# The later modulation units as pairs of half contractions by 512 columns, in another order of the weight stream

## The reference

```
m = silu(cond) @ w_mod + b_mod                    # w_mod is 1024 x 6144
shift1, scale1, gate1, shift2, scale2, gate2 = split(m, 6)
h = rmsnorm(x, g_mix) * (1 + scale1) + shift1
... = split(h @ w_in)                             # inputs of four token mixers
branches = [retention, window attention, differential attention, latent attention]
branches = einsum('blnc,ncd->blnd', branches, w_branch)      # n: the mixer
gates = sigmoid(h @ w_gate + b_gate)                         # 4 x 1024 columns
mixed = sum(gates * branches, axis=mixer) @ w_out
x = x + gate1 * mixed
h2 = rmsnorm(x, g_ffn) * (1 + scale2) + shift2
x = x + gate2 * mlp(h2)                           # gated, with a convolution of width 3
```

## Time and profile before

| what | value |
| --- | --- |
| median of 3 runs | 2319.7 us (2318.75 to 2321.82) |
| profiled execution, its own time | 2321.85 us |
| its span | 2319.7 us |
| busy: PE, PEld, DVE, ACT, POOL | 99%, 89%, 55%, 40%, 32% of the span |
| moved by DMA | 221.62 MB, 96 GB/s on the mean |

### The profile page before, as it was taken

One profiled execution on the slowest core, in us unless ns is written; L12 is line 12 of the kernel. 1 busy time (PEld: TensorE's weight loads), 2 busy tenths in 40 slices (PEclk: granted clock), 3 DMA queues, 4 the chain that ended last, 5 costly groups with the idle time before them and its releaser, 6 DMA issues.

```text
span 2319.7 us, 40593 instructions
## 1 busy us (share of the span) xinstructions
PE 2287.5 (99%) x17116; PEld 2062.1 (89%) x17116; DVE 1275.7 (55%) x2234; ACT 924.5 (40%) x1763; POOL 750.1 (32%) x498
## 2 busy tenths in 40 slices
PE   7999999999999999999999999999999999999998
PEld 5888898888989998998988879888889899899897
DVE  4436458644336763763664373685444467547556
ACT  3335346634335331331362452555442443223223
POOL 0331221211433544544422303121123435544442
PEclk9999999999999999999999999999999999999999
DMA  9413222223242324223232142222232322222211
GB/s 317 139 57 121 76 95 81 78 74 107 100 127 73 91 91 128 73 91 123 78 137 75 39 134 92 85 67 92 74 110 84 108 91 74 76 70 78 87 60 68
DMA packets 221906, 221.62 MB, mean 96 GB/s; under 512 B 10582, under 2 KB 191390, under 8 KB 221470
## 3 DMA queue, kind: packets, MB, share of 16 engines
q1 hardware_dynamic: 212999, 193.77, 26.2%
q10 hardware_dynamic: 8727, 25.27, 3.2%
HBM read 209.90 MB, written 9.11 MB: 94 GB/s over the span
## 4 chain that ended last, share of the span: by engine, by line
PE 93%; DVE 3%; ACT 3%; issue 1%; POOL 1%; DMA 0%; SPq 0%; POOLq 0%; DVEq 0%; ACTq 0%
PE ps L896 50%; PE ps L1027 12%; PE ps L1564 11%; PE ps L1486 4%; PE ps L1168 3%; PE ps L1185 2%; PE ps L916 2%; PE ps L1129 1%; PE ps L1144 1%; PE ps L992 1%; PE ps L1114 1%; PE ps L1388 1%; PE ps L1150 1%; PE ps L907 1%; POOL w_lo L855 1%
## 5 line engine op out<-in xcount | busy, mean ns | idle before, releaser
L855 POOL TENSOR_TENSOR w_lo<-raw,w_hi 128x512 fp32r<-128x512 f32 (+1 forms) x486 | 739.9, 1552 | 1547.6 <-ACT w_hi L1636 992.8
L896 PE MATMUL ps<-h_hi,w_hi 128*128 128x320 f32 (+2 forms) x2368 | 615.2, 312 | 0.0
L896 PE MATMUL ps<-h_hi,w_lo 128*128 128x320 f32 (+2 forms) x2368 | 607.2, 309 | 0.0
L896 PE MATMUL ps<-h_lo,w_hi 128*128 128x320 f32 (+2 forms) x2368 | 606.6, 309 | 0.0
L896 PEld LDWEIGHTS ps<-h_hi,w_hi 128*128 128x128 f32 x2368 | 413.4, 188 | 7.1 <-issue 4.6
L896 PEld LDWEIGHTS ps<-h_lo,w_hi 128*128 128x128 f32 x2368 | 413.4, 188 | 0.2
L896 PEld LDWEIGHTS ps<-h_hi,w_lo 128*128 128x128 f32 x2368 | 412.9, 188 | 0.0
L1636 ACT ACTIVATE w_hi<-raw 128x2048 fp32r<-128x2048 f32 (+2 forms) x110 | 203.7, 1852 | 268.7 <-PE ps L1564 95.0
L2650 DVE TENSOR_SCALAR conv<-u_pad,vcol 128x642 f32<-128x642 f32 x88 | 90.1, 1023 | 151.1 <-ACT u_pad L2072 149.5
L1564 PE MATMUL ps<-w_hi,a_hi 128*128 128x512 f32 x440 | 172.3, 392 | 0.6 <-POOL w_lo L855 0.6
L1564 PE MATMUL ps<-w_lo,a_hi 128*128 128x512 f32 x440 | 171.3, 389 | 0.0
(11 more groups left out here) (348 smaller groups left out, 3475.8 us busy)
## 6 DMA issues: line engine op xcount, KB each, us to landing
raw<-in_w_mod SPq DMA_DIRECT2D x44, 1024.0 KB, 5.1
raw<-in_w_up SPq DMA_DIRECT2D x88, 512.0 KB, 4.8
raw<-in_w_gate SPq DMA_DIRECT2D x32, 1024.0 KB, 5.4
raw<-in_w_in SPq DMA_DIRECT2D x16, 1024.0 KB, 5.1
raw<-in_w_down SPq DMA_DIRECT2D x16, 1024.0 KB, 5.0
w_br<-in_w_branch ACTq DMA_DIRECT2D x8, 1024.0 KB, 5.0
raw<-in_w_out SPq DMA_DIRECT2D x8, 1024.0 KB, 5.6
raw<-in_w_down SPq DMA_DIRECT2D x8, 768.0 KB, 4.4
```

The lines of the kernel that those rows point to most:

```text
L855: ins = nc.gpsimd.tensor_tensor(w_lo[part_slot(li, s)][:, c0:c1], raw[HOME[u]][:, c0:c1], w_hi[part_slot(li, s)][:, c0:c1].bitcast(F32), A ...
L896: ins = mm(out, w_at(w_hl[wi]), at_(x_hl[xi]), start=first and q == 0, stop=final and q == 2)
```

## The change

Units 8 to 23 become eight pairs. A pair covers 512 columns, and its two 1 MB loads are the two halves of the contraction (512 rows by 512 columns each, 128x4x512 in the buffer) and no longer two ranges of 256 columns. `mod_halves` computes a pair in one filler: all 32 products have 128 columns, four column groups each take the whole contraction for 128 of the 512 columns, and the second half adds to the first. `take_halves` on the vector engine transposes the blocks within PSUM and adds the bias for all 512 columns. `mod_unit`, `mod_direct`, `mod_transpose`, `take_row`, `take_mod` and `take_direct` go, with `mod_row` and its constant. The pairs stand in steps 2, 11 and 17 of stage 1, 2 and 10 of stage 2, and 2, 10 and 20 of stage 3. The weight stream is rearranged to match; when a stage's gate weights are rounded (`ROUND_AT`) stays as it was.

```
-    units += gate(0, 2) + mods(1) + gate(0, 3) + mods(3) + [("in", (3, 0), True, li)] + mods(2) + [("in", (3, 1), True, li)] + win(4) + win(5)
-    units += gate(1, 0) + gate(1, 1) + mods(2) + gate(1, 2) + mods(1) + gate(1, 3) + mods(1) + gate(2, 0)
-    units += [("uq", 0, False, li)] + gate(2, 1) + [("ukv", 0, False, li)] + mods(2) + gate(2, 2) + mods(1) + gate(2, 3)
-    units += mods(2) + gate(3, 0) + mods(1) + gate(3, 1) + gate(3, 2) + gate(3, 3)
+    units += gate(0, 2) + mods(2) + gate(0, 3) + [("in", (3, 0), True, li)] + mods(2) + [("in", (3, 1), True, li)] + mods(2) + win(4) + win(5)
+    units += gate(1, 0) + gate(1, 1) + mods(2) + gate(1, 2) + gate(1, 3) + mods(2) + gate(2, 0)
+    units += [("uq", 0, False, li)] + gate(2, 1) + [("ukv", 0, False, li)] + mods(2) + gate(2, 2) + gate(2, 3) + mods(2)
+    units += gate(3, 0) + mods(2) + gate(3, 1) + gate(3, 2) + gate(3, 3)
...
-        return [[gate(10)], [branch(0), gate(11)], [branch(1)], [branch(2), mod(0)], [row(0), branch(3)], [gate(12)],
-                [branch(4), mod(1)], [branch(5), row(1)], [branch(6), mod(2)], [branch(7), row(2)], [branch(8), gate(13)], [branch(9), mod(3)],
-                [row(3)], [branch(10)], [branch(11), mod(4)], [branch(12), row(4)], [], [branch(13), mod(5)], [row(5)],
+        return [[gate(10)], [branch(0), gate(11)], [branch(1), mod(1)], [branch(2)], [branch(3)], [gate(12)],
+                [branch(4)], [branch(5)], [branch(6)], [branch(7)], [branch(8), gate(13)], [branch(9), mod(3)],
+                [], [branch(10)], [branch(11)], [branch(12)], [], [branch(13), mod(5)], [],
                 [gate(14)], [gate(15)], [branch(14)], [branch(15)]]
...
-    for k, where in enumerate((5, 13, 21, 29) if br == 2 else (5, 13, 21, 29, 35, 41)):
-        items[where:where] = [mod(k), row(k) if at + k < DIRECT_MOD else None]
+    pairs = {5: mod(1), 21: mod(3), 41: mod(5)}
+    for where in (5, 13, 21, 29) if br == 2 else (5, 13, 21, 29, 35, 41):
+        items[where:where] = [pairs.get(where), None]
...
+                def mod_halves(q):
+
+                    c0 = mod_col(q)
+                    for half in range(2):
+                        w = raw_unit("mod", 2 * q + half)
+                        for k4 in range(4):
+                            k = 4 * half + k4
+                            turns = w[:, k4, :].rearrange("p (b g j) -> p g b j", g=4, j=32)
+                            for g in range(4):
+                                last = mm(ps[32 * g:32 * g + 32, c0:c0 + P].rearrange("p (b j) -> p b j", j=32),
+                                          cond_c[:, k, 2:34], turns[:, g], start=k == 0, stop=k == KD - 1)
+                        last.then_inc(mod_mm.sem, 1)
...
+                def take_halves(q):
+
+                    ve.wait_ge(mod_mm.sem, now(mod_mm, 2 * q + 2))
+                    V.transpose(ps[:, mod_col(q) + P:mod_col(q) + 2 * P], ps[:, mod_col(q):mod_col(q) + P]).then_inc(vstep.sem, 1)
                     ve.wait_ge(vstep.sem, step())
...
+                    tt(mod[:, 4 * q:4 * q + 4, :], ps[:, mod_col(q) + P:mod_col(q) + 2 * P].rearrange("p (b r) -> p b r", b=4)[:, :, 0:2],
+                       vcol[:, BMOD + 4 * q:BMOD + 4 * q + 4].unsqueeze(2).to_broadcast([P, 4, 2]), ALU.add).then_inc(mod_done.sem, 1)
```

More of the change, by code:

```diff
@@ L521, in build @@
         vec_t, vec_done = Signal("vectors_transposed"), Signal("vectors_ready")
-        mod_mm, (row_done, mod_t) = Signal("mod_product", 24), (Signal(n, DIRECT_MOD - 8) for n in ("mod_row_ready", "mod_transposed"))
+        mod_mm = Signal("mod_product", 24)
         ahead_done = Signal("modulation_ahead", 4)
         mvec_t, mvec_done = Signal("mod_vectors_transposed"), Signal("mod_vectors_ready")
-        mod_done, scl_done = Signal("mod_ready", 20), Signal("scale_ready", 5)
+        mod_done, scl_done = Signal("mod_ready", 12), Signal("scale_ready", 5)
         squared, rms_done, rstd_done, xn_done = Signal("row_squares"), Signal("row_rms"), Signal("row_rstd"), Signal("row_normed")
@@ L673, in left_bank @@
             kind, q = item
-            if kind == "mod" and q >= DIRECT_MOD:
-                return mod_done, q - 3
-            return {"gate": (g_out, q + 1), "branch": (b_read, q + 1), "mod": (row_done, q - 7), "mod_row": (mod_done, q - 3)}[kind]
+            return {"gate": (g_out, q + 1), "branch": (b_read, q + 1), "mod": (mod_done, q + 1)}[kind]
         block = ctx.enter_context(nc.Block())
@@ L684, in unit_source @@
             cut = lambda ap: ap.rearrange("l (k p) n -> p (l k) n", p=P)
+            if kind == "mod" and i >= 8:
+                return cut(a["w_mod"][one, i % 2 * 512:(i % 2 + 1) * 512, i // 2 * 512:(i // 2 + 1) * 512]), 4, 512
             if kind == "mod":
@@ L708, in unit_cols @@
             return k * n
-        unit_shape = [(kind,) + {"mod": (8, 256), "uq": (2, 384), "ukv": (1, 512), "gate": (8, 256),
+        unit_shape = [(kind,) + {"mod": (4, 512) if kind == "mod" and i >= 8 else (8, 256), "uq": (2, 384), "ukv": (1, 512), "gate": (8, 256),
                                  "out": (4, 512), "up": (8, 256), "in": (4, G_COLS[i[0]][1] if kind == "in" else 0),
@@ L897, in product3 @@
                     return ins
[L899 to L908, removed]
                 def mod_rows(layer, i, c0):
@@ L942, in mod_ahead @@
                     mod_rows(li + 1, MOD_ORDER[n], ahead_col(n))
[L944 to L951, removed]
                 def turn_channels(k):
@@ L1100, in fill @@
                         pe.wait_ge(sig.sem, now(sig, count))
-                    mod_form = mod_direct if item[0] == "mod" and item[1] >= DIRECT_MOD else mod_unit
-                    {"gate": gate_chunk, "branch": branch_chunk, "mod": mod_form, "mod_row": mod_transpose}[item[0]](item[1], **part)
+                    {"gate": gate_chunk, "branch": branch_chunk, "mod": mod_halves}[item[0]](item[1], **part)
                 def attention(br, ahead=None):
@@ L1310, in _ @@
                 pe.wait_ge(b_read.sem, now(b_read, 16))
-                pe.wait_ge(mod_done.sem, now(mod_done, 10))
+                pe.wait_ge(mod_done.sem, now(mod_done, 7))
                 in_product(4)
@@ L1352, in slot @@
                         pe.wait_ge(b_read.sem, now(b_read, 32))
-                        pe.wait_ge(mod_done.sem, now(mod_done, 14))
+                        pe.wait_ge(mod_done.sem, now(mod_done, 9))
                     if k >= 4:
@@ L1455, in _ @@
                 pe.wait_ge(b_read.sem, now(b_read, 48))
-                pe.wait_ge(mod_done.sem, now(mod_done, 20))
+                pe.wait_ge(mod_done.sem, now(mod_done, 12))
                 for v in range(2):
@@ L1651, in round_quarter @@
                         nxt[0] += 1
[L1653 to L1658, removed]
                 def row_rms(which, t, junk):
@@ L1833, in attention @@
                         for kind, q in filling(br, i):
-                            if kind == "mod" and q < DIRECT_MOD:
-                                take_row(q)
                             if kind == "gate":
@@ L2387, in attention @@
                                 take_branch(q)
[L2388 to L2391, removed]
+                            if kind == "mod":
+                                take_halves(q)
                 if li:
@@ L2598, in _ @@
                 attention(3)
-                ve.wait_ge(mod_done.sem, now(mod_done, 20))
+                ve.wait_ge(mod_done.sem, now(mod_done, 12))
                 scale(1, 0, 8)
```

21 lines of the change are left out of this document (2 added, 19 removed).

## The result

The changed kernel is slower: 2330.09 us median of 4 runs (2328.49 to 2334.86) against 2319.77 us for the kernel before (4 runs), a ratio of 1.0043 with a 95% interval of 1.0031 to 1.0056. That is +10.3 us where +5.6 was forecast; the median lies at the upper edge of the range, 2330. The profiled execution took 2331.03 us, its span is 2329.2 us.

The account below looks back on a forecast made before the run. The tensor engine, 99% busy, was taken as the bound, with the softmax chain close behind. Stages 1 to 3 gave 1.9 + 1.4 - 0.5 = +2.8 us a layer, +5.6 for two: 2325.3 us against 2319.7, range 2318.0 to 2330.

Parts of the forecast that it names:

- The price of the pair: Time from a pair's start to the next tensor product: 1.89 us, between 1.78 and 2.00, against a later unit's 1.03 or 1.00.
- The sum of stage 1: All step terms of the first attention stage together: +1.9 us a layer.
- steps 2 to 6: Stage 1, the pair moved to step 2: its take delays head 3, a new wait of 0.85, +1.27 us a layer.
- Two pairs stand where units stood (steps 2 and 10): Stage 2: two pairs cost +1.72 us, units removed from steps 6 and 14 give -0.01 and -0.28; +1.4 a layer.
- What costs nothing: The vector engine's takes of later stages are shorter in total and lie under gate products, so they add no time.
- Here the work counts in full: Stage 3: scores come every second step, so removed units gain fully: 3 x 0.86 - 3 x 1.03 = -0.5 us a layer.
- the prices' own range: Spread of the forecast from unknown prices of the pair, steps 8 to 10 and the takes: 2322.3 to 2328.3 us.
- a late weight: Rival, slower: gate (0,3) lands after 169.45, lateness paid once a layer; 2 us a layer more is 2329.3; chance 0.03.
- the tensor engine did not stay the bound: Rival, faster: the tensor engine bounds throughout and 4.0 us a layer is saved, 2311.7 us; chance 0.10.
- the late takes did show: Rival, no change: two late takes do not hold the scores of steps 4 and 14, 2321.6 us; chance 0.33.
- the pair does not go by its instruction count: Rival, faster: priced by instruction count, a pair costs a unit's 1.03, 0.86 less, 16 times: 2311.5 us; chance 0.03.

Follow-up runs that it names:

- e1_pool_later: The changed kernel with one more wait on GpSimd, for gate unit (1,3) in stage 2, until the normalising is done: 2328.5 us, ratio 1.0027.
- e5_hold_stage3: The changed kernel with GpSimd held for gate unit (2,2) until head 6 of stage 3 is normalised: 2329.1 us, ratio 1.0033.
- e7_take_later: The changed kernel with the takes of stage 1's first two pairs moved from steps 2 and 11 to 3 and 13: 2326.4 us, ratio 1.0019.
- both mixtures: Pairs in stage 1 (steps 3, 13, 17 or 3, 9, 15) and stage 3, stage 2 as before, GpSimd held for (2,2): ratios 0.9977 and 0.9968.
- e6_best: The changed kernel with pairs in steps 9, 13, 17 (stage 1) and 6, 14 (stage 2), GpSimd held for gate units (1,3) and (2,2): 2334.6 us.
- e9_hybrid: Pairs in stage 1 (3, 13, 17) and stage 3 (2, 10, 20), stage 2's single units as before, GpSimd held for (2,2): 2316.6 us, ratio 0.9977.

## Why the prediction came out as it did

The direction and the mechanism were right: filler taken from steps in which the scores hang on the softmax chain comes back as waiting, and takes put in front of a head make new waits. The price of the pair, 1.89, was measured as 1.89 (379.35 to 381.24). The sum of stage 1 was +1.9 and is +2.1; steps 2 to 6 were 0.25 short, and the rest agrees within 0.1. Of the 0.25, some 0.18 is the turn ahead of the pair: before, branch product 2 started 0.02 after it, and the pair starts 0.20 after it.

Two steps were mis-sized, both by the same omission. "Two pairs stand where units stood (steps 2 and 10)" gave +1.4 for stage 2, which is +3.1: I priced the pair on the tensor engine alone, and "What costs nothing" put the takes of the later stages at nothing because they lie under gate products. The longer pair also starts the vector engine's normalising 0.9 later against ScalarE's rounding, which is enough for GpSimd to be first; `e1_pool_later` shows that this is all of the missing 1.77. "Here the work counts in full" gave -0.5 for stage 3, which is 0.0: at step 6 only 0.30 of 1.03 was gained, since there the sum of a branch product and the normalising ran into GpSimd, as `e5_hold_stage3` shows. Together 2.2 us a layer, 4.4 of the 4.7 that were missing. The trace of before had the sign of it: at 381.93 and 382.97 the same two operations, of another head, lasted 1.00 and 1.78 with GpSimd at work, in a place where nothing waited. That the median still lies at the edge of the range is luck: the prices' own range ended at 2328.3, and the rest up to 2330 was left for a late weight, which did not come.

Of the rivals, the tensor engine did not stay the bound, the late takes did show (`e7_take_later`), the pair does not go by its instruction count, and no weight came late.

What stays open is the clock. In the profiled runs the stretches at the lower level account for the difference between spans and steps; over all runs the mean granted clock has a median of 0.997 in both mixtures and 0.996 in the kernel before, and a thousandth of the span is 2.3 us. By this estimate the clock explains most of the 2.7 and 3.3 us by which times and steps differ. Whether the mixtures cause this, and how, no run here shows, since none holds the clock fixed.

## What to carry to other kernels

An engine that is busy for 99% of the span may still have a second chain just under it: before taking work away, read at each place how much earlier than the engine's own work the second chain ends, because only that much is a gain. When a product is made longer or moved, ask not only who waits for it but which operations of the consumer will then run beside GpSimd, and whether the other side of that race moves too. And check a new place against the ring of buffers: the next unit in the stream may be waiting for the buffer that the moved one still holds.

## What the runs showed of the hardware

The granted clock was below full in single stretches of some microseconds. In the traces of this case they come again at a few places (about 22, 154, 439 to 449, 1303 to 1309 and 1586 to 1594 us, and at the end of the span, besides the stalls of `e6_best`), and which of these places have one differs from trace to trace. Windows of the kernel before, of the changed one and of `e9_hybrid` (length, busy time of PE, PEld, DVE, ACT and POOL with their instructions, then the granted clock, DMA share, GB/s):

```profile
150.00:160.00 10.00, 10.00 (x58) 8.55 (x57) 3.01 (x4) 2.68 (x3) 3.84 (x3) 1.00 0.25 85
...
1584.00:1594.00 10.00, 10.00 (x58) 9.17 (x58) 5.88 (x26) 6.94 (x12) 0.00 (x0) 0.83 0.18 71
```

```profile
150.00:160.00 10.00, 10.00 (x51) 8.51 (x50) 2.86 (x4) 2.68 (x3) 4.65 (x4) 0.83 0.14 54
...
1595.00:1605.00 10.00, 10.00 (x69) 8.67 (x70) 6.47 (x29) 8.39 (x15) 0.57 (x1) 1.00 0.27 93
```

```profile
1577.00:1587.00 10.00, 10.00 (x72) 9.31 (x71) 4.63 (x20) 8.40 (x15) 0.00 (x0) 1.00 0.31 107
```

The two levels are 2.4 and 1.2 GHz, so 0.83 over 10 us is some 3.4 us at the lower one and costs 1.7 us; the tensor engine was busy in all five windows. Ahead of the window at 1584 it was busy for 23.25 of 24 us; what brings such a stretch on is not shown. Between the same products the changed kernel lost 1.66 us less at the second place. Such stretches shift a single run of this kernel by as much as many of its steps are worth, while the shifts of scores starts within a stage repeat within 0.1 us from run to run.
